# Hyena transforms over even and odd tokens, tokens loaded back beside the pairs, and half of the second-key tables on GpSimd

## What is computed

```
def run_layer(layer, x, cvec, s0_f, s0_b, P):
    sh1, sc1, g1, sh2, sc2, g2 = modulation(cvec, P['w_mod'][layer], P['b_mod'][layer])
    h = layer_norm(x) * (1.0 + sc1) + sh1
    y = ab_mixer(...) if layer % 2 == 0 else hyena_mixer(h, layer // 2, P)
    x = layer_norm(DN_ALPHA * x + g1 * y, P['ln_mix_g'][layer], P['ln_mix_b'][layer])
    h = layer_norm(x) * (1.0 + sc2) + sh2
    y = peer(h, layer, P)
    return layer_norm(DN_ALPHA * x + g2 * y, ...)

def long_conv(u, h_f, h_b, skip):          # L = 128 and L = 512
    taps = jnp.concatenate([h_f, jnp.zeros((1, D), F32), h_b[:0:-1]], axis=0)
    uf = jnp.fft.rfft(u, n=2 * L, axis=1)
    tf = jnp.fft.rfft(taps, axis=0)
    return jnp.fft.irfft(uf * tf[None], n=2 * L, axis=1)[:, :L] + u * skip

def hyena_mixer(h, o, P):
    x0, x1, v = jnp.split(short_conv(h @ P['hy_w_in'][o]), 3, axis=-1)
    y = long_conv((v * x1).astype(F32), h_f, h_b, P['hy_skip'][o])
    return (y * x0) @ P['hy_w_out'][o]

def peer(h, layer, P):
    # q = x @ wq; s1, s2 = scores against 128 first and 128 second keys; top 16 of each,
    # top 16 of their sums: idx (first key * 128 + second key) and gates (softmax)
    act = jax.nn.gelu(jnp.einsum('td,ted->te', xb, u_tab[ib])) * gb
    return jnp.einsum('te,ted->td', act, v_tab[ib])
```

## Time and profile before

| | us |
|---|---|
| median of three runs | 4605.14 |
| profiled execution, its own time | 4605.67 |
| span from its first to its last instruction | 4603.9 |
| busy in the span: TensorE, VectorE (DVE) | 4011.0 (87%), 3557.2 (77%) |
| GpSimd (POOL), ScalarE (ACT) | 1662.0 (36%), 1550.6 (34%) |
| prologue, until the first norm | 0 to 192 |
| gate tables of layer 0, of layer 1 | 1362 to 1494, 3322 to 3455 |
| Hyena spectra, inverse transform | 2856 to 2922, 2922 to 2995 |

### The profile page before, as it was taken

One profiled execution on the slowest core, in us unless ns is written; L12 is line 12 of the kernel. 1 busy time (PEld: TensorE's weight loads), 2 busy tenths in 40 slices (PEclk: granted clock), 3 DMA queues, 4 the chain that ended last, 5 costly groups with the idle time before them and its releaser, 6 DMA issues. The chain is left out here.

```text
span 4603.9 us, 79716 instructions
## 1 busy us (share of the span) xinstructions
PE 4011.0 (87%) x29482; PEld 3290.9 (71%) x29482; DVE 3557.2 (77%) x7212; ACT 1550.6 (34%) x2971; POOL 1662.0 (36%) x1279
## 2 busy tenths in 40 slices
PE   6779999968948899999999589889488999999994
PEld 1346666654946799999999488449477999999994
DVE  3225666653899799999999856338996999999998
ACT  1124444432229333333333231012293333333332
POOL 0001111111330466666666400013303666666665
PEclk8889999988979999999999789989799999999997
DMA  9520000003005999999999522030059999999996
GB/s 359 229 75 18 19 19 19 17 27 137 2 1 146 372 407 398 407 406 406 389 398 394 191 93 87 24 137 2 1 146 354 407 399 407 407 405 390 393 397 233
DMA packets 393991, 1049.25 MB, mean 228 GB/s; under 512 B 37351, under 2 KB 168679, under 8 KB 391656
## 3 DMA queue, kind: packets, MB, share of 16 engines
q0 software_dynamic: 147456, 536.94, 29.7%
q1 hardware_dynamic: 219304, 493.06, 28.7%
q10 hardware_dynamic: 27008, 16.25, 1.2%
HBM read 990.58 MB, written 55.54 MB: 227 GB/s over the span
## 5 line engine op out<-in xcount | busy, mean ns | idle before, releaser
L873 PE MATMUL bank<-h_parts,u_parts 128*128 128x384 f32 x6144 | 1116.3, 336 | 40.8 <-DVE u_parts L968 36.5
L873 PEld LDWEIGHTS bank<-h_parts,u_parts 128*128 128x128 f32 x6144 | 1081.3, 188 | 62.4 <-issue 36.8
L883 PE MATMUL bank<-v_parts,gg_parts 128*128 128x512 f32 x4608 | 1100.2, 392 | 13.2 <-DVE v_parts L988 13.2
L883 PEld LDWEIGHTS bank<-v_parts,gg_parts 128*128 128x128 f32 x4608 | 862.8, 188 | 187.2 <-issue 15.9
L851 POOL DMA_INDIRECT late<-in_peer_v,rows_idx x512 | 618.5, 1208 | 197.7 <-issue 149.6
L957 DVE SCALAR_TENSOR_TENSOR late<-late,yT 128x1024 f32<-128x1024 f32 x512 | 661.0, 1292 | 31.9 <-DMA late<-in_peer_v,rows_idx 17.7
L924 ACT ACTIVATE gg_parts<-late 128x384 fp32r<-128x384 f32 x256 | 133.9, 523 | 1035.7 <-DVE late L978 1019.6
L843 POOL DMA_INDIRECT late<-in_u_rows,rows_idx x256 | 348.6, 1362 | 303.3 <-DVE yT L951 278.1
L843 POOL DMA_INDIRECT hT<-in_u_rows,rows_idx x128 | 213.1, 1665 | 485.8 <-DVE h_parts L943 359.9
L947 DVE TENSOR_TENSOR u_parts<-hT,u_parts 128x1024 fp32r<-128x1024 f32 x256 | 311.7, 1218 | 44.0 <-issue 29.3
L488 PE MATMUL bank<-hT,late 128*128 128x128 f32 x2560 | 314.4, 277 | 8.4 <-PEq L60 8.4
(11 more groups left out here) (355 smaller groups left out, 5787.7 us busy)
## 6 DMA issues: line engine op xcount, KB each, us to landing
yT<-in_peer_v SPq DMA_DIRECT2D x256, 512.0 KB
hT<-in_peer_u SPq DMA_DIRECT2D x256, 512.0 KB
w_modt<-in_w_mod SPq DMA_DIRECT2D x24, 2048.0 KB, 15.6
late<-gates SPq DMA_DIRECT2D x168, 192.0 KB
late<-in_peer_wq SPq DMA_DIRECT2D x32, 512.0 KB, 8.8
gates<-late SPq DMA_DIRECT2D x2, 8192.0 KB, 30.4
gates<-gates_sb SPq DMA_DIRECT2D x2, 8192.0 KB, 30.4
w_raw<-in_hy_w_in SPq DMA_DIRECT2D x24, 512.0 KB, 3.6
```

The costliest lines, as they stand in the source:

```text
L873: mm = pe.matmul(m.bank[j % 2][:, 0:TD], us[:, j % 2, a, k, :], hs[:, b, k, :], start=(k == 0 and i == 0), stop=(k == KD - 1 and i == 2))
L883: mm = pe.matmul(yb[t][c][:, :], gs[:, j, a, t * P:(t + 1) * P], vs[:, j % 2, b, c * BANK:(c + 1) * BANK], start=(first and i == 0), stop= ...
```

## The change

**Transforms.** The 512 latent tokens are split into 256 even and 256 odd ones, in the filters (whose positions are laid out so by the constants), in `H.ut` (the transposes read every second token) and in the outputs. Only 256 frequencies are transformed, each for the even and for the odd tokens; sum and difference give a frequency and its mirror. In the prologue ACT copies the even half and DVE adds and subtracts the odd one (`both_halves`). In `hyena_spectra` ACT copies the even half, DVE makes `plus` and `minus` and their products with the taps at 1 + kt and 3 + kt, and GpSimd sums and differences of the two for `H.y`. In `hyena_back` the result is formed for each parity x from 256 rows, and DVE writes it with a step of two. Both tables are 1152 KB (128 x 2304 floats); both are loaded in `hyena_inputs`.

**Tokens** come back in two halves, issued by SP behind the states of pair 4 and of pair 5; the block for it is gone.

**Gate tables.** GpSimd makes the second-key tables of the first two tokens of a group, DVE those of the last two; ACT makes the fourth token's first-key table only in every second group, DVE in the others.

Core of the diff:

```diff
-        table = [P, QT, NKEY]
+        table = [P, 2, NKEY]
         with nc.Block() as block:
             @block.vector
             def _(dve):
@@ -683,12 +683,22 @@
                     u = k % TBLS
                     if k >= TBLS:
                         dve.wait_ge(s["pg_mm"], k + 1)
-                    dve.tensor_tensor(hot[:, u, 1], selT[:, 1, k * QT:(k + 1) * QT].unsqueeze(2).broadcast_to(table),
+                    dve.tensor_tensor(hot[:, u, 1, QT - 2:QT], selT[:, 1, k * QT + QT - 2:(k + 1) * QT].unsqueeze(2).broadcast_to(table),
                                       m.iota[:, :].unsqueeze(1).broadcast_to(table), ALU.is_equal)
-                    for q in range(QT - 1):
+                    for q in range(QT - 1 + k % 2):
                         t = k * QT + q
                         ins = dve.tensor_scalar(hot[:, u, 0, q, :], m.iota[:, :], selT[:, 0, t:t + 1], selT[:, 2, t:t + 1], ALU.is_equal, ALU.mult)
                     ins.then_inc(s["pg_hot"], 1)
+
+            @block.gpsimd
+            def _(pool):
+                for k in range(BLOCKS * GROUPS):
+                    if k >= TBLS:
+                        pool.wait_ge(s["pg_mm"], k + 1)
+                    for q in range(QT - 2):
+                        t = k * QT + q
+                        ins = pool.tensor_scalar(hot[:, k % TBLS, 1, q, :], m.iota[:, :], selT[:, 1, t:t + 1], None, ALU.is_equal)
+                    ins.then_inc(s["pg_second"], 1)
 
             @block.tensor
             def _(pe):
@@ -698,9 +708,10 @@
                         k = TBLS * r + u
                         pe.wait_ge(s["pg_hot"], k + 1)
                         pe.wait_ge(s["pg_sb"], k + 1)
+                        pe.wait_ge(s["pg_second"], k + 1)
                         for q in range(QT):
-                            if q == QT - 1:
-                                pe.wait_ge(s["pg_last"], k + 1)
+                            if q == QT - 1 and u % 2 == 0:
+                                pe.wait_ge(s["pg_last"], TBLS // 2 * r + u // 2 + 1)
                             mm = pe.matmul(m.bank[u][:, q * P:(q + 1) * P], hot[:, u, 1, q, :], hot[:, u, 0, q, :], start=True, stop=True)
                         mm.then_inc(s["pg_mm"], 1)
...
-                for k in range(3):
+                for k in (0, 2):
...
-                    if k + 3 < BLOCKS * GROUPS:
+                    if k % 2 == 1 and k + 3 < BLOCKS * GROUPS:
...
+                    if p == PAIRS - 2:
+                        sp.dma_start(xs[:, 0:half], tokens[:, 0:half]).then_inc(s["rk_back"], 16)
+                sp.dma_start(xs[:, half:2 * half], tokens[:, half:2 * half]).then_inc(s["rk_back"], 16)
                 sp.wait_ge(s["rk_store"], 32 * PAIRS)
+                sp.wait_ge(s["rk_back"], 32)
...
-        with nc.Block() as block:
-            @block.sync
-            def _(sp):
-                sp.dma_start(m.x[:, :, :], m.tokens).then_inc(s["rk_back"], 16)
-                sp.wait_ge(s["rk_back"], 16)
...
-                        sp.dma_start(H.tab[:, :, :, :], m.i["dft"]).then_inc(s["hi_tab"], 16)
-                sp.wait_ge(s["hi_tab"], 16)
+                        sp.dma_start(H.tab.all, m.i["dft"]).then_inc(s["hi_tab"], 16)
+                    if n == 4:
+                        sp.dma_start(H.back.all, m.i["idft"]).then_inc(s["hi_tab"], 16)
+                sp.wait_ge(s["hi_tab"], 32)
...
-                for k in range(TT):
+                for k in (1, 3, 2, 4, 0):
...
+                        for x in range(2):
+                            for i in range(2):
+                                t = 2 * x + i
+                                mm = pe.matmul(banks(n)[2 * j + x][:, :], H.tab.lat[:, t, j, kt * P:(kt + 1) * P], H.ut[:, 1 + t, h * BANK:(h + 1) * BANK], start=(i == 0), stop=(i == 1))
...
+                    dve.wait_ge(s["hs_even"], n + 1)
+                    for j in range(2):
+                        dve.tensor_tensor(plus[:, j], even[:, j], banks(n)[2 * j + 1][:, :], ALU.add)
+                    if n >= 1:
+                        dve.wait_ge(s["hs_yb"], n)
+                    for j in range(2):
+                        ins = dve.tensor_tensor(minus[:, j], even[:, j], banks(n)[2 * j + 1][:, :], ALU.subtract)
+                    ins.then_inc(s["hs_both"], 1)
                     if h == 0:
-                        dve.wait_ge(s[f"hs_taps{k}"], 16 * 4)
-                    dve.wait_ge(s["hs_mm"], n + 1)
+                        dve.wait_ge(s[f"hs_taps{1 + kt}"], 16 * 4)
+                        dve.wait_ge(s[f"hs_taps{3 + kt}"], 16 * 4)
+                    dve.wait_ge(s["hs_both"], n + 1)
+                    for j in range(2):
+                        ins = dve.tensor_tensor(pa[:, j], plus[:, j], taps[:, 1 + kt, j, sl], ALU.mult)
+                    link(ins)
+                    for j in range(2):
+                        ins = dve.tensor_tensor(plus[:, j], plus[:, j], taps[:, 1 + kt, 1 - j, sl], ALU.mult)
+                    for j in range(2):
+                        ins = dve.tensor_tensor(pb[:, j], minus[:, j], taps[:, 3 + kt, j, sl], ALU.mult)
+                    link(ins)
+                    for j in range(2):
+                        ins = dve.tensor_tensor(minus[:, j], minus[:, j], taps[:, 3 + kt, 1 - j, sl], ALU.mult)
+                    ins.then_inc(s["hs_b"], 1)
                     if n >= 1:
-                        dve.wait_ge(s["hs_y"], 2 * n)
-                    b = 2 * (n % 4)
-                    dve.tensor_tensor(pr[:, 0], m.bank[b][:, :], taps[:, k, 0, sl], ALU.mult)
-                    dve.tensor_tensor(pr[:, 1], m.bank[b + 1][:, :], taps[:, k, 1, sl], ALU.mult)
-                    dve.tensor_tensor(pr[:, 2], m.bank[b][:, :], taps[:, k, 1, sl], ALU.mult)
-                    dve.tensor_tensor(pr[:, 3], m.bank[b + 1][:, :], taps[:, k, 0, sl], ALU.mult).then_inc(s["hs_read"], 1)
-                    dve.wait_ge(s["hs_read"], n + 1)
-                    dve.tensor_tensor(H.y[0][:, k, sl], pr[:, 0], pr[:, 1], ALU.subtract).then_inc(s["hs_y"], 1)
-                    dve.tensor_tensor(H.y[1][:, k, sl], pr[:, 2], pr[:, 3], ALU.add).then_inc(s["hs_y"], 1)
-                dve.wait_ge(s["hs_y"], 2 * len(work))
+                        dve.wait_ge(s["hs_pair"], n)
+                    dve.tensor_tensor(ya[:, 0], pa[:, 0], pa[:, 1], ALU.subtract)
+                    ins = dve.tensor_tensor(ya[:, 1], plus[:, 0], plus[:, 1], ALU.add)
+                    ins.then_inc(s["hs_a"], 1)
+                    dve.wait_ge(s["hs_a"], n + 1)
...
+                    pool.wait_ge(s["hs_b"], n + 1)
+                    if n >= 1:
+                        pool.wait_ge(s["hs_pair"], n)
+                    pool.tensor_tensor(yb[:, 0], pb[:, 0], pb[:, 1], ALU.subtract)
+                    pool.tensor_tensor(yb[:, 1], minus[:, 0], minus[:, 1], ALU.add).then_inc(s["hs_yb"], 1)
+                    pool.wait_ge(s["hs_yb"], n + 1)
+                    pool.wait_ge(s["hs_a"], n + 1)
+                    for j in range(2):
+                        pool.tensor_tensor(H.y[j][:, 1 + kt, sl], ya[:, j], yb[:, j], ALU.add)
+                    for j in range(2):
+                        ins = pool.tensor_tensor(H.y[j][:, 3 + kt, sl], ya[:, j], yb[:, j], ALU.subtract)
+                    ins.then_inc(s["hs_pair"], 1)
...
-                sp.dma_start(tab[:, :, :, :], m.i["idft"]).then_inc(s["hk_tab"], 16)
...
-                pe.wait_ge(s["hk_tab"], 32)
...
+                            for x in range(2):
+                                for kt in range(2):
+                                    for j in range(2):
+                                        mm = pe.matmul(m.bank[i % 4][:, x * HALF:(x + 1) * HALF], H.y[j][:, 1 + 2 * x + kt, sl], H.back.inv[:, kt, j, x * HALF:(x + 1) * HALF],
+                                                       start=(kt == 0 and j == 0), stop=(kt == 1 and j == 1))
...
+                        if c == 1:
+                            u, y = u.rearrange("p (n x) -> p n x", x=2), y.rearrange("p (x n) -> p n x", x=2)
...
+    work = [(0, 0, h, j) for h in range(2) for j in range(2)] + [(1, kt, h, j) for kt in range(2) for h in range(2) for j in range(2)]
...
+                                mm = pe.matmul(m.bank[2 + 2 * (n % 2) + x][:, :], tab.lat[:, t, j, kt * P:(kt + 1) * P], pm[:, 1 + t, j, sl], start=(i == 0), stop=(i == 1))
...
-                    if q == SPECTRA_FROM:
-                        for n in range(2):
-                            for j in range(2):
-                                spectrum(n, j)
-                    if SPECTRA_FROM <= q:
-                        half = q - SPECTRA_FROM
-                        spectrum(2 + half // 2, half % 2)
+                    if SPECTRA_FROM <= q < SPECTRA_FROM + len(work):
+                        spectrum(q - SPECTRA_FROM)
...
+                def both_halves(n):
+                    c, kt, h, j = work[n]
+                    if c == 0:
+                        return
```

(18 more changed lines are left out.)

180 lines of the change are left out of this document (123 added, 57 removed).

## The result

The changed kernel takes 4546.57 us (median of 4 runs, 4545.10 to 4549.76) against 4606.53 for the kernel before in the same comparison: ratio 0.9868, 95% interval 0.9851 to 0.9885. Its profiled execution took 4545.10 us with a span of 4543.0; the kernel before had 4605.67 and 4603.9. The forecast was 4555.

The account below looks back on a forecast made before the run. It took the kernel as a row of barrier-separated blocks, each bound by the engine or transfer ending it. Tokens -9.8, prologue -10, spectra +1, inverse -37, gate tables +5 summed to -50.8: 4555 us, range 4512 to 4612.

Parts of the forecast that it names:

- Tokens: Block loading tokens back before the combine: its load and entry go, -9.8 us, bounds -8 and -11.
- inverse transform: Inverse block: table loaded earlier and matmuls of 256 columns, 36 us against 73.3, -37, bounds -39 and -33.
- Both cost nothing: The two token-load halves, behind pair 4's and pair 5's states, stay hidden; without that cover at most 5 us.
- Prologue: Prologue: fewer spectra matmuls, transfers as the floor, last weights near 168 us; -10 us, bounds -4 and -13.
- Spectra: Hyena spectra: fewer matmuls but a longer elementwise chain, 67.6 against 66.4 us; +1, bounds -12 and +3.
- Gate tables: Gate tables, 192 groups: 1.40 us a group with GpSimd's share against 1.372; +5 us, bounds -26 and +89.
- 0.17 of the 0.30 excludes: Gate tables: part of each GpSimd operation that keeps DVE out; half taken, 0.08 us each.
- rival 3: Gate tables: GpSimd sets the pace, its comparison over 0.69 us; at 1.0, +120, 4670 us; chance 0.08.
- 1.835 a group: Gate tables' upper bound: each GpSimd operation keeps DVE out for its whole 0.30 us, +89 us.
- Rival 1: Short GpSimd operations slip between DVE's and spectra overlap more: gates -26, spectra -5, total 4518 us; chance 0.22.
- rival 2: Gate tables: each GpSimd operation shuts DVE out whole, kernel slower than before at 4639 us; chance 0.13.
- rival 4: Transforms give less than their matmuls say: prologue -4, spectra +3, inverse -33, total 4567 us; chance 0.07.

Follow-up runs that it names:

- Run 10: Repeat of the changed kernel with the prologue's filter spectra four slots later (slots 12 to 23 instead of 8 to 19); 4546.84 us.
- run 6: Changed kernel with the prologue's transform table loaded a second time, 1152 KB more moved; 4552.98 us.
- run 11: Repeat of the changed kernel with the prologue's transform table loaded twice; 4558.10 us.
- run 3: Changed kernel with GpSimd's six operations of each Hyena spectra work moved to VectorE; 4546.85 us, block 71.1 against 72.38.
- run 4: Changed kernel with the Hyena spectra's sums and differences written into the banks, so products read a bank; 4539.62 us, ratio 0.9847.
- run 2: Changed kernel with gate tables left out or altered in six stages; no whole time given; VectorE alone 1.235 us a group against 1.318.
- run 7: Changed kernel with the prologue's filter spectra four slots later (slots 12 to 23 instead of 8 to 19); 4549.59 us.

## Why the prediction was right, and where its terms were off

**Tokens, inverse transform.** -9.8 and -37 were measured as -9.7 and -37.2. Both rested on a stretch in which only one thing happened, and on the duration of a matmul in the same block. "Both cost nothing" was perhaps not quite so: the last pair is about 1.7 us longer with the first half of the tokens ahead of its initial state (85.7 against 84.0). It is not a wait for that state, which landed 8.4 us into the pair and was first read 52.2 us into it. No run took the load out, so the cause stays open.

**Prologue, -10 forecast, -14.3 measured**, past the bound of -13. The time of the last weights came out right (near 168; 167.10), in part by luck: in the kernel before they had landed at 175.9 us and not at about 172, so the transfers gained 8.8 us where the step gave them 4. The half clock cost less (2.58 instead of 3.6 us), so the last slot ended at 169.7 and not at 171.6. What the step left out was the last spectrum's stores behind that slot: 10.6 us of tail became 8.5. The traces with the prologue of before give 191.2 and 192.4, those with the changed one 177.5 to 179.3, so the term is -12 to -15. Run 10 shows that taking the spectrum away from the end is no saving by itself: with it back there the norm came at 178.0, since the weights land 5.0 us earlier and VectorE reaches the last rows only 5.5 us behind the slot's matmuls. That the transfers rule now is in TensorE's idle time ahead of the late slots (4.16, 2.38 and 2.22 us ahead of the last three). A kernel with more to load was later by more than its bytes, with a low clock in both of its traces (runs 6, 11).

**Spectra, +1 forecast, +6.0 measured**, past the bound of +3. The mechanism was right: exclusion for operations with two SBUF inputs, none for those that read a bank (run 3: without GpSimd's part the block is 1.3 us shorter; run 4: reading banks takes 9.3 off). The size was off. The prediction's own terms for a work, 3.2 + 2.4 + 5.1 + 1.9, make 12.6 and not the 12.2 that it went on with, which is 1.6 us over four works. Measured is 13.0: the products wait 3.0 us behind GpSimd's last two and not 1.9, while the two sums beside GpSimd take 2.4 and not 3.2. And the last work holds the context up by 1.25 us more.

**Gate tables, +5 forecast, -9.8 measured.** This is the step that failed, though inside its bounds. "0.17 of the 0.30 excludes", and half of that, came from the earlier trace rows, where both engines read two tensors. The scalar operations here read one. GpSimd's costs VectorE 0.04 each, 0.083 a group (run 2), not 0.165; VectorE's own 1.235 was right to the last digit. GpSimd's own price was wrong the other way: 0.593 instead of 0.301, and 2 x 0.58 = 1.16 a group lies just under VectorE's 1.235. That this did no harm is luck, and rival 3 was nearer than its 0.08 says: a little more, and GpSimd would have set the pace.

**The page on the state buffer.** The prediction took from the Trainium skill ("SBUF — State Buffer", Who interferes with whom) that whoever issues first has the shared ports for the whole instruction, which pointed to 1.835 a group. The measured 1.318 decides against that for GpSimd's scalar operations: 0.593 long, each took 0.04 from VectorE, and a VectorE comparison with two SBUF tensors that began 0.29 us into one was not held up (run 2). The same section says that a VectorE instruction with at most one SBUF input outside the 2-port modes does not contend, and one with two does, with a GpSimd instruction that reads SBUF: the spectra agree with it, 1.28 beside GpSimd for two that read a bank and 3.38 for two that read SBUF twice.

**Rivals.** Rival 1 (gates -26, spectra -5) had the direction in the tables, not the size, and was wrong in the spectra; rivals 2 and 3 did not come, nor did rival 4: prologue and inverse transform gave what was said or more. The forecast of 4555 is 8 us above the median, and so close because errors cancel: tables 15 too high, prologue 4 too high, spectra 5 too low, and 6 too low for what lies in no term (4.1 in the table's two other stretches, 1.5 from the profiled execution to the median).

## What to carry to other kernels

Before work moves from VectorE to GpSimd, count the SBUF tensors that each instruction reads. Where VectorE's had two, GpSimd's work beside it gained nothing (block 72.4 us with GpSimd, 71.1 without); where one of VectorE's inputs lay in a PSUM bank, even by writing an intermediate result there, both ran at full speed (1.29 and 1.27 us). Where the two must exclude each other, let GpSimd start behind VectorE's last such instruction (a work of 9.0 us instead of 10.0).

A block that two limits hold is priced by the later one and by what stands behind it: read what follows the last transfer, the stores too, and not only when it lands.

## What was not expected of the hardware

- With no comparison on VectorE, GpSimd scalar operations of 0.59 us delayed its scalar operations by at most 0.07 (0.335 becomes 0.40), while a GpSimd subtraction of two tensors, 0.61 us, delayed one by 0.3 (0.335 becomes 0.672).
- GpSimd's comparison of 128x128 with a per-partition scalar took 0.593 us alone, its multiply and add on the same shape 0.301.
- In two executions of one kernel (runs 7 and 10) the clock between 60 and 80 us was 0.66 and 1.00, and the first norm came 6.4 us later in the first; the whole executions differ by 2.8. Behind the low clock the DMA share fell to 0.63 (0.96 in the other), as the transfers wait for weight slots that TensorE frees.
